# Two thirds of the adaLN projection moved out of the opening stage, and weight slabs stored contiguously

## The reference

```python
def adaln(cond, w_ada, b_ada):
    m = (jax.nn.silu(cond) @ w_ada + b_ada)[:, None, :]
    return jnp.split(m, 6, axis=-1)

def trunk_layer(...):
    sh1, sc1, gt1, sh2, sc2, gt2 = adaln(cond, w_ada, b_ada)
    h = rmsnorm(x, g1) * (1.0 + sc1) + sh1
    aq, ai, aff, afb, ag, bq, bk, bv, ga, gb = split_columns(h @ w_in)
    o_a, s_f, s_b = hgrn2_mixer(...)              # gated linear recurrence
    o_b = ...                                     # attention
    y = (jax.nn.sigmoid(ga) * (o_a @ w_oa) + jax.nn.sigmoid(gb) * (o_b @ w_ob)) @ w_out
    x = x + gt1 * y
    h2 = rmsnorm(x, g2) * (1.0 + sc2) + sh2
    x = x + gt2 * peer(h2, p_wq, p_keys, p_u, p_v)   # 128 gathered expert rows per token
```

## Time and profile before

| | us |
|---|---|
| median of 3 runs (lowest, highest) | 2833.05 (2831.48, 2841.45) |
| the profiled execution, its own time | 2830.93 |
| span of its trace | 2829.1 |

### The profile page before, as it was taken

How to read it: one execution, slowest core, us unless ns; L and a number is a source line. 1 busy time by engine, 2 the same in 40 slices (tenths; PEclk the granted TensorE clock), 3 DMA queues, 4 the chain that set the end, 5 groups by cost and what they waited for, 6 DMA issues and landing times.

```text
span 2829.1 us, 28267 instructions
## 1 busy us (share of the span) xinstructions
PE 2153.3 (76%) x7009; PEld 1201.2 (42%) x7009; DVE 1699.5 (60%) x4090; ACT 949.3 (34%) x2464; POOL 858.2 (30%) x797
## 2 busy tenths in 40 slices
PE   8788897765567789986957777767777778767777
PEld 3477745655556654473523222323223223323222
DVE  2132178665655647652367776776776777776775
ACT  0312144140033343413114443434434444434433
POOL 0020023632301011200025444344444444434444
PEclk9898999887865579997979999899998999989899
DMA  8564778650023247752449999999999999999998
GB/s 282 188 195 135 231 278 296 247 193 16 16 78 118 91 170 272 261 184 96 162 158 418 402 423 399 373 402 397 381 421 371 396 420 409 400 380 378 389 416 339
DMA packets 201681, 790.95 MB, mean 280 GB/s; under 512 B 12772, under 2 KB 116582, under 8 KB 119622
## 3 DMA queue, kind: packets, MB, share of 16 engines
q0 software_dynamic: 92464, 672.05, 59.8%
q1 hardware_dynamic: 107368, 112.40, 12.3%
q10 hardware_dynamic: 1712, 4.98, 0.5%
HBM read 786.10 MB, written 3.28 MB: 279 GB/s over the span
## 4 chain that ended last, share of the span: by engine, by line
PE 33%; DVE 22%; issue 18%; DMA 15%; POOL 5%; ACT 5%; DVEq 1%; POOLq 0%; ACTq 0%; SPq 0%
PE pa L531 24%; DMA RG<-in_uv,idxs 10%; PE pl L507 4%; DVE PB L1133 3%; DMA HL<-in_uv,idxs 2%; DVE PB L1115 2%; DVE R L1174 2%; PE po L531 2%; PE pa L534 2%; DVE PB L1113 2%; POOL HG L1031 2%; DVE pl L1191 1%; DVE PB L1114 1%; DVE PB L1143 1%; DVE PB L1145 1%
## 5 line engine op out<-in xcount | busy, mean ns | idle before, releaser
L1016 POOL DMA_INDIRECT RG<-in_uv,idxs x288 | 309.2, 1073 | 838.6 <-DVE pl L1191 492.6
L507 PE MATMUL pl<-RING,PB 128*128 128x512 f32 x768 | 409.0, 674 | 189.6 <-ACT PB L830 189.5
L507 PE MATMUL pl<-RG,PB 128*128 128x512 f32 x768 | 378.8, 634 | 109.9 <-ACT PB L830 109.5
L820 ACT ACTIVATE agel<-apre 128x1 f32<-128x1 f32 x640 | 127.5, 199 | 960.2 <-DVE apre L1174 952.6
L1016 POOL DMA_INDIRECT RING<-in_uv,idxs x192 | 249.7, 1301 | 335.6 <-PE pl L507 301.9
L507 PEld LDWEIGHTS pl<-RING,PB 128*128 128x128 f32 x768 | 149.1, 205 | 433.7 <-ACT PB L830 285.1
L531 PE MATMUL pa<-HL,RING 128*128 128x512 f32 x704 | 308.6, 597 | 5.6 <-ACTq L372 5.6
L1174 DVE CUSTOM_DVE_ANT_0 R<-RING,AB 128x1024 f32<-128x1024 f32 x192 | 235.1, 1225 | 108.5 <-DMA RING<-in_uv,idxs 86.7
L1174 DVE CUSTOM_DVE_ANT_0 R<-RG,AB 128x1024 f32<-128x1024 f32 x192 | 230.0, 1225 | 113.0 <-DMA RG<-in_uv,idxs 77.2
L507 PEld LDWEIGHTS pl<-RG,PB 128*128 128x128 f32 x768 | 146.4, 199 | 329.2 <-ACT PB L830 178.1
L830 ACT ACTIVATE PB<-CT,wexp 128x128 f32<-128x128 f32 x512 | 205.6, 402 | 196.5 <-PE pl L507 167.9
(11 more groups left out here) (224 smaller groups left out, 2995.9 us busy)
## 6 DMA issues: line engine op xcount, KB each, us to landing
RING<-in_w_in SPq DMA_DIRECT2D x42, 1024.0 KB, 5.7
RING<-in_w_ada SPq DMA_DIRECT2D x24, 1024.0 KB, 5.3
RING<-in_w_pq SPq DMA_DIRECT2D x16, 1024.0 KB, 5.3
RING<-in_w_out SPq DMA_DIRECT2D x8, 1024.0 KB, 6.4
RG<-in_uv,idxs POOLq DMA_INDIRECT x288, 9.1
RING<-in_w_oa SPq DMA_DIRECT2D x8, 512.0 KB, 3.8
RING<-in_w_ob SPq DMA_DIRECT2D x8, 512.0 KB, 5.8
RING<-in_uv,idxs POOLq DMA_INDIRECT x192, 10.8
```

Source lines behind the costliest of these rows:

```text
L507: last = nc.tensor.matmul(PL[:, c * 512:(c + 1) * 512], DG[:, k % 2, :], bufs[k % len(bufs)][:, D + c * 512:D + (c + 1) * 512], start=Fals ...
L820: A(agel[:, par, k:k + 1], apre[:, par, k:k + 1], ACT.Gelu).then_inc(gel_done, 1)
L1016: nc.gpsimd.indirect_dma_start(out=bufs[b], out_offset=None, in_=uv, in_offset=bass.IndirectOffsetOnAxis(ap=idxs[:, par, k:k + 1], axis=0) ...
```

## The change

Five things change in the program.

1. Only the eight slabs of `sc1` and `sh1` (`NFIRST`) are handled in the adaLN stage.
2. The eight slabs of `sh2` and `sc2` are stored transposed (`col_slabs`: 128 output columns on the partitions, two halves of 1024 weights each). DVE takes them by dot products with the condition spread over all partitions (`CONDB`, a new 1 MB transfer, SiLU on ACT): four dots a slab, 32 in all, behind `normed` and ahead of the mask cast, `forget` and the rows 8 to 15. In the ring they stand between the prompt's projection slabs.
3. The eight slabs of the gates stay on PE, as groups `ada` 8 to 15 behind each `win` slab; each group `mod` follows one slab later.
4. The sums of squares stand behind the eight rows instead of between them.
5. Every slab is stored contiguously (8 KB a partition, 9 KB for `wpq` with its keys), and each is one transfer.

The heart of the diff:

```diff
-ADA_SEGS = [1, 0, 2, 3, 4, 5]
-NADA = 4 * len(ADA_SEGS)
+ADA_SEGS = [1, 0, 2, 5]
+NADA, NFIRST, NCOL = 16, 8, 8
...
-SLABS = ([("ada", n) for n in range(NADA)]
-         + [("winT", w, m) for w in WIN_T for m in range(2)]
-         + [("win", w, a) for w, a in WIN])
+SLABS = [("ada", n) for n in range(NFIRST)]
+for _i, (_w, _m) in enumerate((w, m) for w in WIN_T for m in range(2)):
+    SLABS += [("winT", _w, _m), ("col", _i)]
+for _i, (_w, _a) in enumerate(WIN):
+    SLABS += [("win", _w, _a), ("ada", NFIRST + _i)] + ([("col", 6 + _i)] if 6 + _i < NCOL else [])
+SLABS += [("ada", NADA - 1)]
...
-                if n >= NSLAB:
+                if n >= NSLAB and SLABS[n - NSLAB][0] == "col":
+                    sp.wait_ge(coldot_done, SLABS[n - NSLAB][1] + 1)
+                elif n >= NSLAB:
                     wait_full(sp, last_use(SLABS[n - NSLAB]))
...
+                sp.dma_start(at[:, 0:SLOTW if kind == "wpq" else SLAB], src).then_inc(s, 16)
                 if n == 2:
                     sp.dma_start(XP[:], x_prompt).then_inc(x_in, 16)
                     sp.dma_start(XL, x_sample.rearrange("(t p) d -> p t d", p=P)).then_inc(x_in, 16)
-                if n == NADA:
+                    sp.dma_start(CONDB, cond_rows.rearrange("p (c d) -> p c d", c=2)).then_inc(condb_in, 16)
+                if n == NFIRST + 2:
...
-            win("win", [0])
+            for i, (wc, a) in enumerate(WIN):
+                win("win", [0], wc, a)
+                ada_row(NFIRST + i)
+                if i:
+                    ada_mod(NFIRST + i - 1)
+            ada_row(NADA - 1)
+            ada_mod(NADA - 2)
+            ada_mod(NADA - 1)
...
+            act.wait_ge(condb_in, 16)
+            step(A(CONDB, CONDB, ACT.Silu), condb_ready)
...
             dve.sem_inc(am_ready, 1)
+            dve.wait_ge(x_in, 32)
+            for t in range(NT):
+                ssq(x0(t), t, SQ1)
             for t in range(NT):
                 if t >= 2:
                     wait_full(dve, ("xT", t - 2))
                 normed(t, x0(t), XN1[:, t % 2, :])
+            dve.wait_ge(condb_ready, 1)
+            for i in range(NCOL):
+                slot, count = slab_turn[("col", i)]
+                dve.wait_ge(slab_in[slot], count)
+                for m in range(2):
+                    n = 2 * i + m
+                    for c in range(2):
+                        ins = V.tensor_tensor_reduce(out=CJUNK, in0=RW_[:, slot * SLOTW + m * D:slot * SLOTW + (m + 1) * D],
+                                                     in1=CONDB[:, c, :], scale=1.0, scalar=0.0, op0=ALU.mult, op1=ALU.add,
+                                                     accum_out=ADA[:, 2 + n // KD, c, n % KD:n % KD + 1])
+                        if m and c:
+                            step(ins, coldot_done)
+                        else:
+                            step(ins)
+            for n in range(2):
+                step(V.tensor_tensor(ADA[:, 2 + n], ADA[:, 2 + n],
+                                     CO[:, C_BADA + 8 * (3 + n):C_BADA + 8 * (4 + n)].unsqueeze(1).to_broadcast([P, 2, KD]),
+                                     ALU.add))
+            scale_col(1, C_N2, 3)
             dve.wait_ge(misc_in, 48)
             step(V.tensor_copy(MK[:], MK4), mk_ready)
...
             dve.wait_ge(q_ready, 4)
+            for n in range(NFIRST, NADA):
+                row(n)
...
+    def slabs(w, k):
+        return w.reshape(k, P, -1, SC_W).transpose(2, 1, 0, 3).reshape(-1, P, k * SC_W)
```

More of the change, by code:

```diff
@@ L127, in post @@
             names.append(("ss", b, m))
-    for n in range(NADA + 1):
-        if n < NADA:
+    for n in range(NFIRST + 1):
+        if n < NFIRST:
             names.append(("ada", n))
@@ L135, in plan_groups @@
     names.extend(("winP", w, m) for w in WIN_T for m in range(4))
-    names.extend(("win", w, a, 0) for w, a in WIN)
+    for i, (w, a) in enumerate(WIN):
+        names.extend([("win", w, a, 0), ("ada", NFIRST + i)])
+        if i:
+            names.append(("mod", NFIRST + i - 1))
+    names.extend([("ada", NADA - 1), ("mod", NADA - 2), ("mod", NADA - 1)])
     scan(0)
@@ L431, in build @@
         for n, key in enumerate(SLABS):
-            counts[n % NSLAB] += 32 if key[0] in ("wo", "wpq") else 16
+            counts[n % NSLAB] += 16
             slab_turn[key] = (n % NSLAB, counts[n % NSLAB])
@@ L462, in _ @@
                 kind = key[0]
[L463 to L467, removed]
-                else:
[L469 to L481, removed]
+                if kind == "ada":
+                    src = ada_slabs[ADA_SEGS[key[1] // 4] * 4 + key[1] % 4]
+                elif kind == "col":
+                    src = col_slabs[key[1]]
+                elif kind in ("win", "winL", "winT", "winTL"):
+                    src = in_slabs[key[1] // SC_W + key[2]]
+                elif kind in ("gate_a", "gate_b"):
+                    src = in_slabs[(W_GA if kind == "gate_a" else W_GB) // SC_W + key[2]]
+                else:
+                    src = {"wo": o_slabs, "wout": out_slabs, "wpq": pq_slabs}[kind][key[2]]
+                sp.dma_start(at[:, 0:SLOTW if kind == "wpq" else SLAB], src).then_inc(s, 16)
                 if n == 2:
@@ L539, in _, with ada_row, ada_mod @@
             pe.wait_ge(cond_ready, 1)
[L540 to L546, removed]
-                if n:
[L548 to L558, removed]
+            def ada_row(n):
+                w = chunks(slab("ada", n))
+                ps = start(("ada", n))
+                for k in range(KD):
+                    last = mm(ps[0:2, 0:SC_W], condT[:, :, k], w[:, k, :], k == 0, k == KD - 1)
+                finish(("ada", n), last)
+            def ada_mod(n):
+                pe.wait_ge(grow_ready, n + 1)
+                ps = start(("mod", n))
+                row = GR[n % 2]
+                if ADA_SEGS[n // 4] in GATE_SEGS:
+                    for c in range(2):
+                        last = mm(ps[:, c * SC_W:(c + 1) * SC_W], SEL[:, c, :], row)
+                else:
+                    for m in range(2):
+                        last = nc.tensor.transpose(ps[:, 2 * m:2 * m + 2], row[:, m * P:(m + 1) * P], ident[0:2, 0:2])
+                finish(("mod", n), last)
+            for n in range(NFIRST + 1):
+                if n < NFIRST:
+                    ada_row(n)
+                if n:
+                    ada_mod(n - 1)
             for t in range(NT):
@@ L578, in _, with win @@
             win_turned("winT", "winP", hTp, P)
[L580 to L587, removed]
-            win("win", [0])
+            def win(kind, tiles, wc, a):
+                w = chunks(slab(kind, wc, a))
+                for t in tiles:
+                    ps = start(("win", wc, a, t))
+                    for k in range(KD):
+                        last = mm(ps[:, 0:SC_W], h_tile(t, k), w[:, k, :], k == 0, k == KD - 1)
+                    finish(("win", wc, a, t), last)
+            for i, (wc, a) in enumerate(WIN):
+                win("win", [0], wc, a)
+                ada_row(NFIRST + i)
+                if i:
+                    ada_mod(NFIRST + i - 1)
+            ada_row(NADA - 1)
+            ada_mod(NADA - 2)
+            ada_mod(NADA - 1)
             pe.wait_ge(win_ready[W_I], 2)
@@ L784, in _ @@
             win_turned("winTL", "winT", hTl, LAT)
-            win("winL", range(1, NT))
+            for wc, a in WIN:
+                win("winL", range(1, NT), wc, a)
             pe.wait_ge(win_ready[W_I], 2 * NT)
@@ L873, in _ @@
                 root(t)
-            act.wait_ge(am_ready, 3)
+            act.wait_ge(am_ready, 2)
             for t in range(NT):
@@ L897, in win @@
                     step(A(o, i, fn), *freed(("win", wc, a, t)), win_ready[wc])
-            for wc, a in WIN:
+            for i, (wc, a) in enumerate(WIN):
                 win(wc, a, [0])
+                if i:
+                    gate_rows(NFIRST + i - 1)
+            gate_rows(NADA - 2)
+            gate_rows(NADA - 1)
             def scan(u):
```

66 lines of the change are left out of this document (36 added, 30 removed).

## The result

| | before | after |
|---|---|---|
| median, us (lowest, highest) | 2837.25 (2831.48, 2843.75), 4 runs | 2871.23 (2865.65, 2875.49), 4 runs |
| ratio, 95% interval | | 1.0118 [1.0084, 1.0152] |
| profiled execution, us (span) | 2830.93 (2829.1) | 2865.65 (2863.8) |

A forecast was written before the change was run, and what follows sets the result against it. It took the opening to be one serial path on PE up to the scan. Its terms 4.8 - 1.3 - 1.0 = +2.5 gave 2833.4 for the profiled execution, 2835 us as the median; 8 in 10 range 2819 to 2850.

The forecast's parts named there:

- The front gain: Opening: with eight slabs left in front, projections start at 76.3 instead of 137.0, 60.7 us gone.
- The ring walk: Projections to scan: slab loads through the three-slot ring stall PE and DVE; the scan starts 4.8 us later than before.
- Low clock in the ring: Rival, ring in the opening: PE's pauses bring the low clock, 16-product slabs of 5 or 7 us; chance 0.14.
- Query stage (-1.3): Prompt's query stage: one transfer a `wpq` slab instead of two saves 1.3 us of waiting.
- gathers (-1.0): Beside stage: slab loads free the engines for 8.4 us in all, of which the gathers gain 1.0.
- The expert passes load no slab; nothing is changed there.: Expert passes at the kernel's end: no change in time, so no term in the sum.

The follow-up runs named there:

- the version without the transfer: own buffers plus 102 dummy DVE instructions at the start, with the condition's transfer moved behind the second prompt slab: 2823.18 us, 0.9931.
- own buffers: Kernel after with the eight transposed slabs in three buffers of their own (idle gather buffers) instead of the shared ring: 2842.55 us, 1.0021.
- the layout alone: Kernel before with contiguous slabs, one transfer a slab, and nothing else of the change: 2834.82 us, 0.9999.
- the table moved: Kernel before with the expert table declared as its first input, so that it lies elsewhere in device memory: 2835.19 us, 0.9995.
- the shifts undone: 102 dummy DVE instructions at the start, added to the kernel after (2847.72 us, 1.0028) and to own buffers (2828.67 us, 0.9953).

## Why the prediction was wrong, step by step

- **The front gain (60.7 us).** Measured 57.1. I counted the condition's transfer at nothing. It holds up slab 3 by 1.3 us (26.24 instead of 24.95), and behind that wait, 3.3 us instead of 2.1, the slab runs at a granted clock of 0.68, 5.3 us instead of 3.6. So the last of the eight slabs starts at 43.0 and not at 39.97 "in both kernels"; the other 0.6 are the squares, 8.0 us instead of 7.4. In the version without the transfer the last of the eight starts 4.3 us earlier and the projections at 75.6, near the forecast's 76.3. Some of that is scatter: the same opening gave projections from 77.7 to 80.7 us in other kernels. The stretches of TensorE in the kernel after: first that slab, then the first projection slab, those at 93.85, 108.86 and 117.80, and the run behind the stop (length, then PE's busy time and those of the other engines, clock, DMA share, GB/s):

```profile
26.24:31.60 5.36, 5.36 (x18) 1.75 (x18) 0.01 (x1) 0.80 (x1) 0.00 (x0) 0.68 0.56 234
...
79.95:86.46 6.51, 6.51 (x34) 6.51 (x35) 0.00 (x0) 1.56 (x2) 0.00 (x0) 0.57 0.01 3
93.85:100.23 6.38, 6.38 (x32) 6.19 (x32) 6.05 (x11) 0.28 (x1) 0.00 (x0) 0.58 0.70 259
108.86:114.34 5.48, 5.47 (x32) 5.28 (x32) 3.20 (x7) 0.28 (x1) 0.00 (x0) 0.69 0.79 271
117.80:121.60 3.80, 3.80 (x32) 3.65 (x32) 1.27 (x3) 0.28 (x1) 0.00 (x0) 1.00 0.97 334
151.65:202.20 50.55, 50.55 (x208) 29.58 (x208) 4.02 (x10) 8.07 (x17) 3.21 (x4) 0.94 0.64 213
```

- **The ring walk (+4.8, measured +15.9).** The mechanism was right, down to which load waits for which dots; the term was mis-sized. `winT` 0 ended at 86.5 (81.7 in the walk): 3.7 from the front and 1.1 from the clock. The loads on the path took 4.9, 7.1, 5.9, 4.8 and 4.8 us, where the walk had 4.7, 4.9, 6.3, 4.8 and 4.8. So the price of a load alone was right within 0.2, and the one that was off is that of `winT` 4: it was issued only 1.45 us behind the load of `col` 3, which had waited for `winT` 2, and `winT` 2 had run 6.4 us. The slab of `winT` 4, at 108.86, ran 5.5 us instead of 3.6. So the last dot ended at 145.3 instead of 136.5, and with 0.8 more for what stands between it and `mod` 8 this began at 151.65 instead of 142.1. The run behind it took 50.6, not 47.5, and the hand-over to the scan 1.1 instead of 2.7. Sum: 9.5 + 3.1 - 1.6 = 11 on top of 4.8.
- **Low clock in the ring**, one of the rivals, turned out half true: granted 0.57 in the first slab, 0.58 and 0.69 in those at 93.85 and 108.86, each behind a stop of 3.8 us, 1.00 in the one at 117.80 behind 3.5, and 0.94 over the last run, behind 7.1. The last run's 208 products took 47.9 us at a clock of 1.00 in the kernel with own buffers:

```profile
127.00:174.86 47.86, 47.86 (x208) 27.84 (x208) 4.04 (x10) 8.06 (x17) 3.22 (x4) 1.00 0.72 243
```

So the clock costs that run 2.7 us, of which the walk had 1.8, and the other 2.2 of its 3.1 are work that the walk's sum put too low. Beyond what the walk allowed, the clock is 1.1 + 1.9 + 0.9 = 3.9 us on the path, a third of the 11, and what it did to `winT` 2 comes on top.
- **Query stage (-1.3) and gathers (-1.0).** Not seen: DVE's waits for gathers in the beside stage add up to 51.5 us, and were 50.6 before. From the scan's start to the first latent expert pass the kernel after took 7.7 us longer, inside the 10 that I allowed. Of these 5.4 lie behind `route(0)`, and the two kernels with the layout alone and with the table moved, whose time is that of before, show 5.2 and 4.3 there too: that part belongs to the trace of before, which had a quick middle, and not to the change.
- **"The expert passes load no slab; nothing is changed there."** This is the step that failed. Nothing was changed in their instructions or transfers, but 26 instructions ahead of them moved DVE's loops against the pieces in which its instructions are fetched, and two more of its eight branches back had to wait for them. By the shifts undone, that costs 14 to 19 us (own buffers) and 24 to 26 us (after), more than the rest of the change. The sum had it at nothing. With it undone, the kernel after is at 1.0028, 8 us behind before, near the +2.5 and inside the range. That nearness is in part luck: in its trace the scan is still 13.0 us late (200.5) and the middle 5.5 longer, and it is the expert passes, 6.9 us shorter than in the trace of before for no reason found, that bring it back.
- The Trainium skill, "Runtime: NRT & Kernel Launch", section "Instruction fetch mechanics", states the rule that I had not weighed: an engine holds two pages of its stream, fetches the next by itself, and a taken branch to a page that it does not hold stalls it for a fetch. DVE's loop body has 310 instructions, more than one of that section's pages of 256. The traces agree on the stall: every one of the slow branches above is a branch back, and the waits of DVE behind them are 4.4 to 5.7 us each, with 3.5 for the second ones. They do not agree on the page's size: packets of 8 KB, and a shift of 128 instructions brought every gap back to within 0.1 us at the dots listed.

## What to carry to other kernels

VectorE's loops of 310 instructions had a price that depended on where in the stream they lay: 26 instructions ahead of them were worth 0.5 to 0.9% of the time here, and 64 nothing that could be measured (1.0003). So before an edit of the opening is judged by its total time, compare the "issue" waits behind the loops' branches and the instruction packets, and if they differ, pad the stream until they agree. And two consumers of different speed should not take turns in one ring of slots that is freed in order: here that alone cost 27 us of an opening that had been made 57 us shorter.

## What the runs showed of the hardware that I had not expected

- A branch back in DVE's loop took 0.3 to 0.4 us where no instruction packet was fetched and 5.2 to 6.5 us where one or two were, in a stretch in which the DMA engines are busy at 0.97 of their time. A packet of that queue is 8 KB (99 packets, 0.80 MB).
- A gap between two dots can in part be mended by what follows: against 18.1 us of new stalls stand 13.3 us less of waits for gathers. The passes still lost 11, of which these two leave 6 unexplained.
- Contiguous slabs moved at 360 GB/s instead of 323 in their queue and landed 0.4 us sooner where hardly anything else was loading (median 4.9 instead of 5.3 us from 45 to 110 us, the layout alone), and the time of the whole kernel did not change by 0.2%.
